# Hybrid encoder layer: the running sums of the log decays in fp32r, split in a high and a low part

## The reference, cut to what matters

```
la = log_sigmoid(r @ wr + br) / 16            # a decay for each token, head, key, and direction
cum = cumsum(la over the tokens of a chunk)
q_dec = q * exp(cum);  k_inv = k * exp(-cum)
scores = q_dec @ k_inv.T (masked);  o_intra = scores @ v
state = decay * state + k_end.T @ v;  o_inter = q_dec @ state
```

## Time and profile before

| | |
|---|---|
| median of 3 runs | 617.27 us (614.79 to 620.18) |
| the profiled execution's own time | 615.71 us |
| its span, first to last instruction | 613.9 us |
| TensorE matmul, busy share of the span | 94% |
| VectorE, ScalarE, GpSimd | 43%, 34%, 11% |
| mean granted TensorE clock | 0.996 |

### The profile page before, as it was taken

One profiled execution on the slowest core, in us unless ns is written; L12 is line 12 of the kernel. 1 busy time (PEld: TensorE's weight loads), 2 busy tenths in 40 slices (PEclk: granted clock), 3 DMA queues, 4 the chain that ended last, 5 costly groups with the idle time before them and its releaser, 6 DMA issues.

```text
span 613.9 us, 8650 instructions
## 1 busy us (share of the span) xinstructions
PE 574.1 (94%) x3433; PEld 436.5 (71%) x3434; DVE 266.5 (43%) x590; ACT 209.1 (34%) x406; POOL 67.3 (11%) x105
## 2 busy tenths in 40 slices
PE   3999999999999999999999999999999998867894
PEld 3789989888788888888888865667666664443551
DVE  3737477646445755543362577212112111112337
ACT  3546367555786623322341341111111111101113
POOL 4010000001000001100000122022112211111023
PEclk9999999999999999999999999999999999999998
DMA  7375021722231122288888197999999999999994
GB/s 250 87 254 187 35 70 44 251 92 69 68 104 50 55 68 69 63 316 304 304 317 326 82 346 274 364 416 424 422 424 423 425 422 425 424 426 423 425 422 195
DMA packets 58282, 155.77 MB, mean 254 GB/s; under 512 B 8172, under 2 KB 38148, under 8 KB 45952
## 3 DMA queue, kind: packets, MB, share of 16 engines
q1 hardware_dynamic: 53392, 145.66, 61.8%
q0 software_dynamic: 4720, 9.45, 4.1%
q10 hardware_dynamic: 128, 0.09, 0.0%
HBM read 147.31 MB, written 15.75 MB: 266 GB/s over the span
## 4 chain that ended last, share of the span: by engine, by line
PE 75%; DMA 11%; SPq 5%; DVE 4%; issue 2%; POOL 1%; ACT 1%; POOLq 0%; DVEq 0%; ACTq 0%
PE bank L727 43%; PE bank L1116 12%; PE bank L1137 6%; PE bank L720 5%; SPq L492 5%; DMA slot2a<-expert_w_up 5%; DMA zt<-expert_rows 3%; PE bank L822 1%; DMA expert_rows<-y,zcol 1%; DMA x_in<-x 1%; PE bank L800 1%; PE bank L801 1%; PE bank L925 1%; PE bank L1035 1%; PE bank L938 1%
## 5 line engine op out<-in xcount | busy, mean ns | idle before, releaser
L1116 PE MATMUL bank<-slots,xgT 128*64 128x256 f32 x544 | 76.6, 381 | 4.6 <-DMA slot2b<-expert_w_up 1.9
L1732 DVE TENSOR_TENSOR w_low<-w,w_high 128x1024 fp32r<-128x1024 f32 x32 | 39.2, 1225 | 78.6 <-ACT w_high L1366 78.6
L727 PE MATMUL bank<-x_high,w_high 128*128 128x512 f32 x168 | 66.9, 398 | 1.0 <-DVE x_low L1649 1.0
L1116 PEld LDWEIGHTS bank<-slots,xgT 128*64 128x64 f32 x544 | 51.6, 137 | 21.9 <-issue 3.1
L727 PE MATMUL bank<-x_high,w_low 128*128 128x512 f32 x168 | 65.6, 391 | 0.0
L727 PE MATMUL bank<-x_low,w_high 128*128 128x512 f32 x168 | 65.5, 390 | 0.0
L2037 DVE TENSOR_SCALAR y<-bank,slot_weights 128x512 f32<-128x512 f32 x14 | 10.5, 751 | 91.9 <-PE bank L1137 91.9
L1366 ACT ACTIVATE w_high<-w 128x1024 fp32r<-128x1024 f32 x32 | 33.7, 1054 | 48.6 <-PE bank L727 48.6
L727 PE MATMUL bank<-w_high,x_high 128*128 128x420 f32 x128 | 45.3, 354 | 0.0
L727 PE MATMUL bank<-w_high,x_low 128*128 128x420 f32 x128 | 45.3, 354 | 0.0
L727 PE MATMUL bank<-w_low,x_high 128*128 128x420 f32 x128 | 45.2, 353 | 0.0
(11 more groups left out here) (287 smaller groups left out, 1137.0 us busy)
## 6 DMA issues: line engine op xcount, KB each, us to landing
slots<-expert_w_gate SPq DMA_DIRECT2D x19, 1024.0 KB, 27.8
slots<-expert_w_up SPq DMA_DIRECT2D x17, 1024.0 KB
slots<-expert_w_down SPq DMA_DIRECT2D x16, 1024.0 KB, 25.1
slot2b<-expert_w_down SPq DMA_DIRECT2D x9, 1024.0 KB, 26.8
w<-w_in SPq DMA_DIRECT2D x16, 512.0 KB, 3.6
slot2b<-expert_w_up SPq DMA_DIRECT2D x8, 1024.0 KB
slot2b<-expert_w_gate SPq DMA_DIRECT2D x8, 1024.0 KB, 19.2
w<-w_in SPq DMA_DIRECT2D x8, 840.0 KB, 4.7
```

Of the source, the lines that this page charges most:

```text
L727: ins_ = mm(out_, stat[a_], mov[b_], start=first and q_ == 0, stop=last and q_ == 2)
L1116: ins = mm(bank[2][e * SLOTS:(e + 1) * SLOTS, m * FE:(m + 1) * FE], xgT[:, c, e * SLOTS:(e + 1) * SLOTS], gu[m][e][:, c], start=(c == 0), ...
L1732: V.tensor_tensor(wl2[:, u % 2, :], raw2[:, u % 2, :], wh2[:, u % 2, :].bitcast(F32), ALU.subtract).then_inc(s["lo_done"], 1)
```

## The change

- The two triangles, 128 x 256 numbers in `cst`, are copied once into a tile of type fp32r, `tri_all`. POOL does this after the inverse roots and ahead of the bias transfers, and waits for the constants first and for the copy afterwards.
- `la` is split as the other operands of the kernel are: ACT writes `la_h`, `la` rounded to fp32r, and DVE writes `la_l`, the rest. Both are done block by block, in the steps `("dk", b)`.
- `cum(b)` has, for each direction, two fp32r matmuls into the same bank, over the high and the low part, in place of one fp32 matmul. It waits for `la_h` and `la_l` of its block. `whole_decay` goes on reading `la` in fp32.
- The two semaphores of the fills become one, `zeroed`, with new counts. The sum `both_halves` (L1842) moves from `gate_weights()`, after unit 7, to after unit 13. `la_h` lies in room that was kept free behind the states, and `la_l` where `yb_high` lies later.

```
+        la_h = v3(place_at(at_ + NT * 512, "la_high", NT * 512, F32R), 512)
...
+        la_l = v3(place_at(YB, "la_low", NT * 512, F32R), 512)
...
+        tri_all = place_at(END_ALL, "triangles", 2 * P, F32R)
+        tri_r = [tri_all[:, i_ * P:(i_ + 1) * P] for i_ in range(2)]
...
                 inverse_root(rstd[:, t:t + 1], ss[:, t:t + 1], D).then_inc(s["rstd_done"], 1)
+            pool.wait_ge(s["const_in"], 16)
+            nc.gpsimd.tensor_copy(tri_all[:, :], cst[:, CONST["triF"][0]:CONST["triB"][1]]).then_inc(s["zeroed"], 1)
+            pool.wait_ge(s["zeroed"], 3)
             pool.wait_ge(s["vrow_done"], 1)
...
                 if b == 0:
                     pe.wait_ge(s["abs_done"], NT)
+                    pe.wait_ge(s["zeroed"], 3)
+                pe.wait_ge(s["la_hi"], b + 1)
+                pe.wait_ge(s["la_done"], NT + 2 + b + 1)
                 if b >= 2:
                     pe.wait_ge(s["ecum_done"], 2 * (b - 1))
                 for d, tri in enumerate(("triF", "triB")):
-                    ins = mm(heads(bank[2 + b % 2][:, :], d), K[tri], heads(la[:, b, :], d), start=True, stop=True)
+                    for q_, part in enumerate((la_h, la_l)):
+                        ins = mm(heads(bank[2 + b % 2][:, :], d), tri_r[d], heads(part[:, b, :], d),
+                                 start=(q_ == 0), stop=(q_ == 1))
                 ins.then_inc(s["cum_done"], 1)
...
+            def la_high(b):
+                act.wait_ge(s["la_done"], NT + 1 + b // 2)
+                A(la_h[:, b, :], la[:, b, :], ACT.Copy).then_inc(s["la_hi"], 1)
...
                 elif name == "dk":
+                    la_high(i)
                     if i == NT - 1:
                         decays()
...
+            def la_low(b):
+                dve.wait_ge(s["la_hi"], b + 1)
+                dve.wait_ge(s["la_done"], NT + 2)
+                V.tensor_tensor(la_l[:, b, :], la[:, b, :], la_h[:, b, :].bitcast(F32), ALU.subtract).then_inc(s["la_done"], 1)
...
+                elif name == "dk":
+                    la_low(i)
```

More of the change, by code:

```diff
@@ L314, in hybrid_encoder @@
             rt_done lr_hi lr_lo z_done abs_done ln_done la_done dk_done dec_done cum_done ecum_done kd_done
-            gt_done gt_out kt_out sc_done sc_out s_zero u_done u_out st_done o_done o_sq silu_done yt_in yt_done yb_hi yb_out
+            gt_done gt_out kt_out sc_done sc_out zeroed u_done u_out st_done o_done o_sq silu_done yt_in yt_done yb_hi yb_out
             gate_done br_done sig_done mul_done merged out_used wo_done x2_done hn_done hn_out
             hT_done hnT_outA hnT_outD rl_done lt_out rl_out rexp_in rexp_done selb_done cb_done rank_done hot_done first_done tab_done cnt_done tabs_done act_done
-            xg_zero zcol_done gathered0 gathered1 gathered2 xt_done xgt_outA xgt_outD gate_in0 gate_in1 gate_in2 gate_in3 up_in0 up_in1 up_in2 up_in3 down_in0 down_in1 down_in2 down_in3 g_done u2_done silu2_done h_done ht_done hTs_done dn_done
+            la_hi zcol_done gathered0 gathered1 gathered2 xt_done xgt_outA xgt_outD gate_in0 gate_in1 gate_in2 gate_in3 up_in0 up_in1 up_in2 up_in3 down_in0 down_in1 down_in2 down_in3 g_done u2_done silu2_done h_done ht_done hTs_done dn_done
             y_outA y_outD scattered0 scattered1 gcolm_done moe_done f_add f_last out_done
@@ L507, in _ @@
             sp.wait_ge(s["lo_done"], 2 * len(jobs))
-            sp.wait_ge(s["xg_zero"], 1)
+            sp.wait_ge(s["zeroed"], 1)
             FREE = 18
@@ L602, in _ @@
             nc.gpsimd.memset(half[:], -0.5).then_inc(s["mean_done"], 1)
-            nc.gpsimd.memset(nil_rows, 0.0).then_inc(s["xg_zero"], 1)
-            nc.gpsimd.memset(wr3[0:96, :].bitcast(F32), 0.0).then_inc(s["s_zero"], 1)
+            nc.gpsimd.memset(nil_rows, 0.0).then_inc(s["zeroed"], 1)
+            nc.gpsimd.memset(wr3[0:96, :].bitcast(F32), 0.0).then_inc(s["zeroed"], 1)
             def inverse_root(dst, sums, n):
@@ L623, in _ @@
             pool.wait_ge(s["exp_done"], NI)
-            nc.gpsimd.memset(rT[0:32, :].bitcast(F32), 1.0).then_inc(s["s_zero"], 1)
-            nc.gpsimd.memset(rT[32:64, :].bitcast(F32), 0.0).then_inc(s["s_zero"], 1)
-            nc.gpsimd.memset(rT[64:96, :].bitcast(F32), 1.0).then_inc(s["s_zero"], 1)
+            nc.gpsimd.memset(rT[0:32, :].bitcast(F32), 1.0).then_inc(s["zeroed"], 1)
+            nc.gpsimd.memset(rT[32:64, :].bitcast(F32), 0.0).then_inc(s["zeroed"], 1)
+            nc.gpsimd.memset(rT[64:96, :].bitcast(F32), 1.0).then_inc(s["zeroed"], 1)
             pool.wait_ge(s["pv_done"], NT)
@@ L629, in _ @@
             for k, zeros in enumerate((st[0:GK, 0, :], st[GK:P, NT - 1, :])):
-                pool.wait_ge(s["s_zero"], k + 4)
-                nc.gpsimd.memset(zeros, 0.0).then_inc(s["s_zero"], 1)
+                pool.wait_ge(s["zeroed"], k + 6)
+                nc.gpsimd.memset(zeros, 0.0).then_inc(s["zeroed"], 1)
             for b in range(NT):
@@ L642, in _ @@
             for k in range(2):
-                nc.gpsimd.memset(xg[k], 0.0).then_inc(s["xg_zero"], 1)
-            pool.wait_ge(s["xg_zero"], 3)
+                nc.gpsimd.memset(xg[k], 0.0).then_inc(s["zeroed"], 1)
+            pool.wait_ge(s["zeroed"], 10)
             def gather(t, n, k, prev):
@@ L1376, in rT_evac @@
                 act.wait_ge(s["rt_done"], 1)
-                act.wait_ge(s["s_zero"], 4)
+                act.wait_ge(s["zeroed"], 6)
                 for at in (0, 64):
@@ L1381, in wr_high @@
             def wr_high():
-                act.wait_ge(s["s_zero"], 1)
+                act.wait_ge(s["zeroed"], 2)
                 for at in (0, 32):
@@ L1735, in wr_low @@
             def wr_low():
-                dve.wait_ge(s["s_zero"], 1)
+                dve.wait_ge(s["zeroed"], 2)
                 dve.wait_ge(s["lr_hi"], 1)
@@ L1740, in rT_low @@
             def rT_low():
-                dve.wait_ge(s["s_zero"], 4)
+                dve.wait_ge(s["zeroed"], 6)
                 dve.wait_ge(s["lr_hi"], 4)
@@ L1806, in u_evac @@
                 if b == 0:
-                    dve.wait_ge(s["s_zero"], 6)
+                    dve.wait_ge(s["zeroed"], 8)
                 for rows, n in ((slice(0, GK), b + 1), (slice(GK, P), b - 1)):
@@ L1841, in gate_weights, with half_sums @@
                 link(ins_)
+            def half_sums():
                 V.tensor_tensor(both_halves[:, :], K["ident"][:, 0:NG + EXPERTS], K["ident"][:, HALF:BOTH], ALU.add
@@ L1905, in _ @@
                         gate_weights()
+                    if i == 13:
+                        half_sums()
                     if i == NF - 2:
```

## The result

The changed kernel took 621.61 us in the median of 13 runs (620.05 to 625.67), the kernel before 616.97 (614.43 to 620.18, 13 runs): ratio 1.0087, 95% interval 1.0069 to 1.0105. It is slower, by 4.6 us on the medians. The ratio is taken over all runs and not from the two medians, whose quotient is 1.0075; by the ratio the difference is 5.4 us. The forecast was +3.0 and 620.3, rival A +5.3.

The account below looks back on a forecast made before the run. The prediction took TensorE to bound the front, with its microseconds reaching the end one for one. Stall +4.6, passes -1.6 and triangles 0 gave +3.0 us, 620.3 us on the median, range 616.0 to 624.3.

Parts of the forecast that it names:

- rival A: TensorE's gap before cum(0) also drops its clock to half, so the pause costs more than its length: 622.6 us, chance 0.33.
- The bound: TensorE bounds the front and starts the experts' loads, so the front's microseconds count one for one at the end.
- Rival C: At SyncE's wait in L505, a fixed row of DMA transfers hides the front's lateness: 617.3 us, chance 0.12.
- The passes: In cum, four fp32r passes at 0.115 us replace four at 0.215, saving 0.40 us per block, 1.6 us in all.
- rival B: In cum, fp32r passes with gaps in the moving operand stay at 0.215 us, saving nothing: 621.9 us, chance 0.07.
- The stall: Before cum(0), TensorE waits for block 0's split of la, queued behind ScalarE's silu: a loss of 4.6 us.
- The other blocks and the triangles: Splits of blocks 1 to 3 lie beside TensorE's work, and POOL's triangle copy in its idle gap: both taken as 0.
- the clock's: Behind the gap before cum(0), TensorE's clock was taken as staying full, adding 0 us to the forecast.
- the likeliest case: Stall before cum(0), saving in the passes and full clock together: +3.0 us, 620.3 us, chance 0.44.

Follow-up runs that it names:

- e1_early: The changed kernel with the high and low parts of blocks 0 and 1 made earlier, at the end of unit 3; ratio 0.9974 to the kernel before, 615.45 us.
- e2_silu_later: The changed kernel with the silu put behind the high parts of blocks 0 and 1 on ScalarE; ratio 1.0037 to the kernel before, 618.83 us.
- e8_work_ahead: The changed kernel with half 5, dk 2 and dk 3 put ahead of cum(0) in TensorE's order; ratio 0.9997 to the kernel before, 616.13 us.
- e5_early_fp32: The changed kernel with the splits of blocks 0 and 1 at the end of unit 3 and the old fp32 matmul; ratio 1.0000 to the kernel before, 617.25 us.
- e4_fp32: The changed kernel, splits and waits kept, with the fp32 matmul on la and fp32 triangles of before; ratio 1.0114 to the kernel before, 623.82 us.
- e7_filler_short: The changed kernel with 8 unused matmuls of 512 columns ahead of the wait in cum(0); ratio 1.0078 to the kernel before, 621.87 us.
- e3_filler: The changed kernel with 19 unused matmuls of 512 columns ahead of the waits in cum(0); ratio 1.0053 to the kernel before, 620.56 us.

## Why the prediction was right, and where it was not

**The bound.** Right. TensorE's front decides, and SyncE's first load that waits moved with it, by 5.3 us (5.0 us at the piece of 411 matmuls, both with the 0.4 us from before the step). Rival C, that the ring swallows it, is out: the table has no kernel where it did.

**The passes.** Right. 0.47 us for four passes in place of 0.86 (0.46 forecast), 0.58 in place of 0.97 in the first block: 1.6 us in all, and e1_early's 0.9974 is that. The gaps in the moving operand cost nothing that shows, so rival B is out.

**The stall.** Right in place, cause and size: 4.51 us (4.6 forecast), behind the silu. The copy took 0.53 us in the chain (0.64) and the subtraction 0.70 (0.69). e2_silu_later shows that the silu with its table load is the cause, and e8_work_ahead that the order of TensorE's queue turns it into a loss.

**The other blocks and the triangles.** Right: e5_early_fp32 has the four splits and the copy and is at 1.0000, and in the changed kernel TensorE has no gap ahead of any later L913.

**The step that failed: the clock's.** The forecast of 620.3 took it as staying full, with a chance of 0.44 against 0.33 for rival A. It fell, in this kernel and in three others. The measured 621.6 lies within the stated range because the range took in rival A; the likeliest case was short by a term that it had put at nothing. The reason given against it was that the one fall in the trace came 3.8 us after the last work, so that a gap of 4.6 us had little room. In the changed kernel it came some 1.1 us after the last matmul (179.4 to 180.5), in e4_fp32 and e2_silu_later 1.4 us after it, and in e7_filler_short 3.9 us after the last unused matmul, when TensorE had been at work again for 1.1 us. One fall was read as a fixed delay. Three of these gaps stand behind 1.7 us of matmuls of 2 columns, the one of e7_filler_short behind matmuls of 512; what the narrow ones do for the clock was not tried by itself, so why the fall came earlier than at the program's end stays open.

Rival A was thus the case that happened, with a size too large: 2.3 us forecast, 1.6 measured in cum(0) and half 5. It was taken as half of the whole 4.6 us of the opening; here the lower level held from 180.5 to 187.3, but only the last 3.4 us of it fell on work. The granted clock of the profile reads 1.00 at the opening too; that the lower level held there is read from the transposes, which start 0.22 us apart at first and 0.12 us apart later. The rule of the Trainium skill, "TensorE: Matmul & The Clock Gate", Part 1, that an idle engine is put to half its rate and has to earn the full one again, agrees: 0.50 in the windows behind the gap, 1.00 again 3.4 us after work began. It did not hold of every pause, as the last section shows. With the measured 1.6 us the sum would have been 3.0 + 1.6 = 4.6 us, which is the lateness of the front; that it is the difference of the medians to the tenth is luck, since the ratio gives 5.4.

## What to carry to other kernels

A cheap preparation step costs nothing or everything by its place in its engine's queue: look at what stands ahead of it there at the moment when the consumer needs it, not at how long it takes. The same change is 0.9% slower with the copies behind a silu and 0.26% faster with them 7 us earlier in the idle time of the same engine. Beside the length of a gap of TensorE of about 2 us or more, carry 1.3 to 1.6 us for the clock as a case of its own: all four such gaps in the front cost it, but in the expert stage of the same traces most gaps of 1.9 to 2.5 us did not. Where ready work stands behind a wait, put it ahead of the wait: e8_work_ahead has the front some 5 us earlier than the changed kernel, e3_filler's unused matmuls some 1.5.

## What the runs showed of the hardware

- In the front the clock fell with gaps of 1.9, 2.8 and 4.5 us, and did not with 0.2, 0.4 and 0.76 us. It need not fall inside the gap: with 2.8 us it fell 1.1 us after work had begun again.
- A gap of 2 us does not decide it. In the expert stage of the ten traces, after 500 us, TensorE has 31 gaps of 1.88 to 2.54 us. The clock fell at 11 of them, in seven of the traces, and stayed full at 20; at the 64 gaps between 0.7 and 1.87 us it never fell. What makes the difference was not tested. One of each kind, from the kernel before and the changed kernel, the clock in the third number from the end of a window:

```profile
551.25 3.65 PE L1137 MATMUL bank<-slots,hT 128*64 128x512 f32 x16 [2.36 <-issue]
552.00:554.00 2.00, 2.00 (x12) 0.83 (x10) 0.00 (x0) 0.69 (x1) 0.01 (x1) 1.00 1.03 434
```

```profile
527.46 0.43 PE L1128 MATMUL bank<-slots,xgT 128*64 128x256 f32 x1 [1.93 <-DMA slot2b<-expert_w_up]
528.00:530.00 2.00, 2.00 (x16) 1.23 (x14) 0.00 (x0) 0.00 (x0) 0.31 (x1) 0.66 1.00 422
```

- The traces are one execution of each kernel, but the mean granted clock of the other executions is on record too. Its median is 0.987 to 0.990 in the four kernels whose traced front lost the clock, and 0.992 to 0.994 in the other six. The fall in the front of the changed kernel, 6.8 us at half clock, takes 0.0055 off the mean of an execution. So it was in all likelihood no accident of the traced executions; the falls in the expert stage lower the same mean, which keeps this from being a proof.
- Gaps of 64 columns in the moving operand of an fp32r matmul of 256 columns cost nothing that shows: 0.47 us for four passes, as by the gapless rows of the attention.
- GpSimd copied 128x256 to fp32r in 0.40 us, where 0.7 was estimated from a sum.
